# Moving the compressed-attention chain of a sparse-attention layer in between the query projections

## The chip, the cores and the metric

The kernel runs on one core of one Trainium2 chip. The metric is the time of one execution in device microseconds (us); lower is better. The kernel before takes 2796.18 us, the median of three runs (2793.33 to 2796.22).

## The reference

The program is a chain of four blocks, all in float32, on 512 tokens of width 1024: a convolution layer with a feed-forward layer, a sparse-attention layer with a feed-forward layer, and then two mixing layers with memory attention and feed-forward layers. The change is in the sparse-attention layer alone. Cut to what matters there:

```python
# from the stream after the convolution layer
kv = rmsnorm(h, kv_norm) @ w_kv        # k_cmp_raw, v_cmp_raw, k_slc, v_slc, k_win, v_win; 2 groups x 64
def compress(raw, pos, w1, w2):        # 31 overlapping blocks of 32 tokens
    blk = raw[:, :, idx] + pos
    return silu(blk.reshape(B, 2, 31, 32 * 64) @ w1) @ w2
k_cmp, v_cmp = compress(k_cmp_raw, ...), compress(v_cmp_raw, ...)

proj = rmsnorm(x, norm_g) @ w_in       # 16 heads x 64 queries, and 3 x 16 gates
gates = sigmoid(proj[..., 1024:])
# for each of 16 heads
p_cmp = softmax(q @ k_cmp.T * scale - slope * dist) * (a block is visible)
o = g[0] * p_cmp @ v_cmp + g[1] * attention(q, k_slc, v_slc) + g[2] * attention(q, k_win, v_win)
h = h + o @ w_out
```

With 8 blocks of 64 tokens and 16 to be chosen, every block is chosen, so that the selected branch is plain causal attention.

## The kernel before

Every stage is a class with one method per engine (`tensor` for TensorE, `vector`, `scalar`, `gpsimd`, `sync` for the queue that loads weights). `plan` lists the stages; each engine runs through its own methods of all stages in that order, and semaphores tie the engines together. Within an engine nothing is reordered. So the order in which stages and calls are written sets everything around the change.

Dense products run in three passes (`three`, lines 211 to 213): weights and activations are each split into a rounded high part and a low remainder, and high x high, high x low and low x high are added. A panel of weights (128 x 1024) is loaded to `raw`, its high part is made on ScalarE (`split_high`, L188) and its low part on VectorE (`split_low`, L194), four panels ahead of the product that uses it. One product is 24 matmuls of 128x512, and VectorE reads its bank out.

The layer's stages before, in order:

- `KeysValues`: six products of keys and values. Between them, ScalarE and VectorE also split the normed stream for the queries into `xb_high` and `xb_low` (L1334, eight slices).
- `CompressBlocks` (VectorE alone): adds the positions, which gives `cmp_blocks` (L1413, four additions).
- `Project` "w_q": eight query products, evicted by VectorE to `queries` (L1051). Each covers a pair of heads.
- `Gates`: one product of 48 columns (weights `w_gates`), sigmoid on ScalarE, transposition (L1498).
- `StackQueries`: ScalarE rounds all queries at once (L1637), VectorE takes the remainder (L1642).
- `Compress`: the hidden layer of the compression (L1450, 128 small matmuls, which the profile records as 256), silu, the second map (L1459, L1464), and VectorE's copies to `cmp_keys` and `cmp_values` (L1426, L1435).
- `StackKeys`: high and low part of the keys (L1659, L1668).
- `CompressedAttention`: scores for group 0 and 1 (L1551), a softmax for each group on VectorE and ScalarE (L1598 to L1617, exponential L1570), values transposed (L1304) and kept (L1313).
- `BranchAttention`: 32 rounds, two heads times two branches for each of eight pairs. Step s of TensorE is the scores of round s (L1755, L1756), the transposition of the probabilities of round s-2 (`turn`, L1773) and their product with the values of round s-3 (`weigh`, L1795); the first `weigh` of a pair begins with the compressed branch (L1788). VectorE adds the distance bias and takes the maximum (L1862), scales two pieces of the probabilities (L1841) and copies a transposed piece (L1846); ScalarE takes the exponential (L1806) and copies (L1813); GpSimd scales the other two pieces (L1730). The compressed probabilities are transposed in steps 0 and 1 (L1562) and copied by ScalarE (L1574).

## Time and profile before

| | |
|---|---|
| median of the runs | 2796.18 us (2793.33 to 2796.22) |
| the profiled execution | 2795.92 us |
| its span in the trace | 2794.1 us |
| TensorE busy | 2656.0 us, 95% of the span |
| VectorE busy | 1404.7 us, 50% |
| ScalarE busy | 942.2 us, 34% |
| GpSimd busy | 348.7 us, 12% |
| mean granted TensorE clock | 0.965 |

The chain that ended last is 87% TensorE and 8% VectorE. The last query product ends at about 718 us of the span, the gate product at 723.5, and the first transposition of the branch attention begins at 781.1 us; its rounds are regular from 788 to 922 us. A clock of 1.00 in a row is TensorE's full 2.4 GHz, 0.50 is 1.2 GHz.

### The profile page before, as it was taken

How to read it: one execution, taken by the hardware profiler on the slowest of the kernel's cores; microseconds unless marked ns; L12 is line 12 of the kernel's file. 1: busy time of each engine (PE TensorE's matmuls, PEld its weight loads, DVE VectorE, ACT ScalarE, POOL GpSimd, SP SyncE). 2: the span in 40 equal slices, each digit the busy share in tenths (PEclk: the TensorE clock that was granted, in tenths of full speed). 3: DMA queues.
4: the chain of work that ended last, by engine and by line, in shares of the span. 5: the costliest groups of instructions: out<-in, count | busy, mean ns of one | idle time of the engine just before them, and what ended most of it. 6: DMA issues, size and time to landing. Idle time of an engine off the chain costs nothing.

```text
span 2794.1 us, 34029 instructions
## 1 busy us (share of the span) xinstructions
PE 2656.0 (95%) x12132; PEld 2154.5 (77%) x12132; DVE 1404.7 (50%) x2125; ACT 942.2 (34%) x1645; POOL 348.7 (12%) x312
## 2 busy tenths in 40 slices
PE   6988999999889999999989898999999999899999
PEld 5866888877777788888768686788887877688887
DVE  5885544335577544433443565544433656544422
ACT  4554332222366332322233533332222124323221
POOL 2002000110055400012100040200011050200000
PEclk9999999999799999999998998999999998999999
DMA  4201333233200133323321022233322322133322
GB/s 144 75 1 61 100 96 96 75 107 117 65 1 1 46 98 97 93 73 105 100 80 34 16 75 77 69 97 98 92 83 99 99 92 91 46 98 98 94 94 68
DMA packets 61007, 219.83 MB, mean 79 GB/s; under 512 B 7137, under 2 KB 7393, under 8 KB 60401
## 3 DMA queue, kind: packets, MB, share of 16 engines
q1 hardware_dynamic: 58896, 209.15, 24.0%
q0 software_dynamic: 2016, 9.44, 1.0%
q8 instruction: 57, 0.93, 0.1%
q14 instruction: 38, 0.30, 0.0%
HBM read 216.47 MB, written 2.10 MB: 78 GB/s over the span
## 4 chain that ended last, share of the span: by engine, by line
PE 87%; DVE 8%; ACT 2%; issue 2%; POOL 0%; DMA 0%; DVEq 0%; ACTq 0%; SPq 0%; POOLq 0%
PE psum L211 25%; PE psum L213 25%; PE psum L212 25%; DVE conv_out L846 2%; PE psum L1795 2%; PE psum L1773 1%; DVE wl L194 1%; PE psum L1157 1%; PE psum L1209 1%; ACT wh L188 1%; PE psum L1755 1%; PE psum L1756 1%; PE psum L2580 1%; PE psum L1976 1%; DVE xl L747 1%
## 5 line engine op out<-in xcount | busy, mean ns | idle before, releaser
L211 PE MATMUL psum<-xh,wh 128*128 128x512 f32 x1880 | 744.3, 396 | 49.3 <-DVE wl L194 23.0
L212 PE MATMUL psum<-xl,wh 128*128 128x512 f32 x1880 | 739.3, 393 | 0.0
L213 PE MATMUL psum<-xh,wl 128*128 128x512 f32 x1880 | 738.8, 393 | 0.0
L188 ACT ACTIVATE wh<-raw 128x1024 fp32r<-128x1024 f32 x404 | 421.0, 1055 | 793.9 <-PE psum L213 792.0
L194 DVE TENSOR_TENSOR wl<-raw,wh 128x1024 fp32r<-128x1024 f32 x404 | 535.7, 1338 | 261.5 <-ACT wh L188 260.7
L211 PEld LDWEIGHTS psum<-xh,wh 128*128 128x128 f32 x1880 | 357.0, 190 | 129.6 <-DVE xl L747 28.6
L213 PEld LDWEIGHTS psum<-xh,wl 128*128 128x128 f32 x1880 | 356.6, 190 | 76.9 <-issue 0.7
L212 PEld LDWEIGHTS psum<-xl,wh 128*128 128x128 f32 x1880 | 357.0, 190 | 74.6 <-issue 0.6
L211 PE MATMUL psum<-hidden_high,wh 128*128 128x512 f32 x704 | 279.2, 397 | 0.0
L212 PE MATMUL psum<-hidden_low,wh 128*128 128x512 f32 x704 | 279.1, 396 | 0.0
L213 PE MATMUL psum<-hidden_high,wl 128*128 128x512 f32 x704 | 279.0, 396 | 0.0
L692 POOL TENSOR_TENSOR square<-x 128x512 f32 (+1 forms) x72 | 79.3, 1102 | 1240.8 <-DVE x L742 1023.5
L712 ACT ACTIVATE xh<-x,cols (+1 forms) x72 | 52.2, 724 | 457.0 <-DVE x L742 426.2
L742 DVE TENSOR_TENSOR x<-psum,x 128x512 f32 (+1 forms) x72 | 49.5, 688 | 310.8 <-PE psum L213 310.8
L578 DVE TENSOR_TENSOR up<-psum,rstd 128x512 f32<-128x512 f32 x96 | 66.4, 691 | 262.5 <-PE psum L213 262.5
L211 PEld LDWEIGHTS psum<-hidden_high,wh 128*128 128x128 f32 x704 | 132.5, 188 | 34.1 <-DVE wl L194 1.7
L213 PEld LDWEIGHTS psum<-hidden_high,wl 128*128 128x128 f32 x704 | 132.6, 188 | 32.3
L212 PEld LDWEIGHTS psum<-hidden_low,wh 128*128 128x128 f32 x704 | 132.6, 188 | 31.5
L555 ACT ACTIVATE hidden_high<-up 128x512 f32 x88 | 55.6, 632 | 175.8 <-DVE up L589 175.8
L569 DVE TENSOR_TENSOR pre<-psum,rstd 128x512 f32<-128x512 f32 x96 | 66.4, 691 | 75.6 <-PE psum L213 74.4
L1730 POOL TENSOR_SCALAR probs<-probs,small 128x512 f32<-128x512 f32 x64 | 92.0, 1446 | 86.5 <-DVE small L1836 86.4
L593 DVE TENSOR_TENSOR hidden_low<-up,hidden_high 128x512 f32 x88 | 61.0, 693 | 81.8 <-ACT hidden_high L555 81.8
(381 smaller groups left out, 3363.8 us busy)
## 6 DMA issues: line engine op xcount, KB each, us to landing
raw<-ffn_in SPq DMA_DIRECT2D x176, 512.0 KB, 3.5
raw<-ffn_out SPq DMA_DIRECT2D x64, 448.0 KB, 4.1
raw<-ffn_out SPq DMA_DIRECT2D x32, 512.0 KB, 3.5
raw<-pw SPq DMA_DIRECT2D x24, 512.0 KB, 3.6
raw<-o_w_hgg SPq DMA_DIRECT2D x12, 512.0 KB, 4.3
raw<-w_q SPq DMA_DIRECT2D x8, 512.0 KB, 3.8
raw<-w_o SPq DMA_DIRECT2D x8, 512.0 KB, 3.6
raw<-e_w_qk SPq DMA_DIRECT2D x8, 512.0 KB, 3.6
```

The lines of the kernel that those rows point to most:

```text
L188: self.nc.scalar.activation(self.wh[:, slot, :], self.raw[:, slot, :], ACT.Copy).then_inc(self.weights_high.sem, 1)
L194: self.nc.vector.tensor_tensor(self.wl[:, slot, :], self.raw[:, slot, :], self.wh[:, slot, :].bitcast(F32), ALU.subtract).then_inc(self.we ...
L211: nc.tensor.matmul(out, ah, bh, start=start, stop=False)
L212: nc.tensor.matmul(out, ah, bl, start=False, stop=False)
L213: return nc.tensor.matmul(out, al, bh, start=False, stop=stop)
L569: dve.tensor_tensor(c.pre[:, r, :], c.psum[:, bank, :], c.rstd[:], ALU.mult).then_inc(c.banks_freed.sem, 1)
L578: dve.tensor_tensor(c.up[:, r, :], c.psum[:, bank, :], c.rstd[:], ALU.mult).then_inc(c.banks_freed.sem, 1)
L593: dve.tensor_tensor(self.hidden[1][:, at, :], c.up[:, r:r + 1, :], self.hidden[0][:, at, :].bitcast(F32), ALU.subtract).then_inc(self.read ...
L692: pool.tensor_tensor(c.square[:, m % 2, :].rearrange("p (a n) -> p a n", a=1), c.x[:, at, :], c.x[:, at, :], ALU.mult).then_inc(self.squar ...
L846: dve.scalar_tensor_tensor(out, taps, w, out, ALU.mult, ALU.add).then_inc(self.tapped.sem, 1)
L1730: pool.tensor_scalar(p, p, self.stat(3, n)[:, i:i + 1], None, ALU.mult).then_inc(self.scaled_wide.sem, 1)
L1795: mm = pe.matmul(acc[:, t * P:S], self.kv.values[:, b, t, g, window], self.pt[n % self.TURNED][t], start=False, stop=(n % 4 == 3 and t == ...
```

## The change

The compression, the gates, the stacking and the compressed attention stop being stages of their own. `Gates`, `StackedKeys` and `CompressedAttention` become plain helpers, and a new stage `Queries` calls their parts between its eight query products. No matmul is added or removed; the dense products, their panels and their bytes are the same.

- `KeysValues.vector` makes `cmp_blocks` at its last two products. `cmp_pos` is loaded first, under a semaphore of its own.
- TensorE: gate product, hidden layer, query product 0, second map, product 1, transposition of gates and values, product 2, and from then on the compressed scores of one pair of heads behind each product.
- ScalarE and VectorE split the queries pair by pair, and the keys at products 2 and 3. The first softmax runs at products 6 and 7.
- The scores of the last pair, and the whole second softmax, move into `BranchAttention`: VectorE does one piece of it at the end of steps 1, 2, 3, 5, 6 and 7, and the remainder of the last two pairs of queries in steps 4 and 8. Its transpositions come at steps 9 and 10.
- Tiles change places; `probs` and `probs_second` now lie in the arena, the key parts where `ssq`, `square`, `pre` and `up` are.

```diff
 class KeysValues(Stage):          # vector, behind product j
             self.low(dve, j)
+            if j >= 4:
+                self.comp.blocks(dve, j - 4)
...
 class Compress(Stage):
+    def gpsimd(self, pool):
...
+        pool.dma_start(self.pos[:], c.dram["cmp_pos"]).then_inc(self.pos_loaded.sem, 16)
+        for t, n in ((self.w1, "phi_w1"), (self.w2, "phi_w2")):
...
 class CompressedAttention:
+    def load(self, pool, g):
+        if g == 0:
+            pool.wait_ge(self.comp.hidden.sem, 1)
+        else:
+            pool.wait_ge(self.added.sem, g)
+        pool.dma_start(self.bias[:].rearrange("p i (h n) -> p i h n", h=8),
+                       c.dram["cmp_bias"][:, :, 8 * g:8 * g + 8, :]).then_inc(self.loaded.sem, 16)
...
+class Queries(Stage):
...
+    def tensor(self, pe):
+        self.gates.product(pe)
+        self.comp.hidden_layer(pe)
+        for j in range(KD):
+            self.product(pe, j)
+            if j == 0:
+                self.comp.map(pe)
+            if j == 1:
+                self.gates.turn(pe)
+                pe.wait_ge(self.comp.kept.sem, 12)
+                self.kv.turn(pe)
+            if j >= 2:
+                self.cmp.score_pair(pe, j - 2)
+            if j == KD - 1:
+                self.cmp.score_pair(pe, KD - 2)
...
+    def scalar(self, act):
+        self.gates.sigmoid(act)
+        self.comp.silu(act)
+        for j in range(KD):
+            c.ahead(c.split_high, act, self.panel0, j, 0, KD)
+            if j >= 1:
+                self.round(act, j - 1)
+            if j == 2:
+                for k in range(4):
+                    self.keys.round(act, k)
+            if j == 4:
+                self.kv.keep(act, self.keys)
+                act.preload_act_table(ACT.Exp)
+            if j == KD - 1:
+                self.cmp.exp(act, 0)
+        self.round(act, KD - 1)
     def vector(self, dve):
+        self.gates.logits(dve)
+        for j in range(KD):
...            # evict product j to queries
+            c.ahead(c.split_low, dve, self.panel0, j, 0, KD)
+            if j == 0:
+                self.comp.keep(dve)
+            if j == 1:
+                self.gates.keep(dve)
+            if 1 <= j <= KD - 2:
+                self.low(dve, j - 1)
+            if 2 <= j <= 3:
+                self.keys.low(dve, 2 * j - 4)
+                self.keys.low(dve, 2 * j - 3)
+            if j == KD - 2:
+                self.cmp.add(dve, 0)
+                self.cmp.maximum(dve, 0)
+                self.cmp.centre(dve, 0)
+            if j == KD - 1:
+                self.cmp.total(dve, 0)
+                self.cmp.share(dve, 0)
+                self.cmp.scale(dve, 0)
...
 class BranchAttention(Stage):     # tensor
             if s < self.ROUNDS:
                 self.score(pe, s)
-            if s < 2:
-                self.cmp.turn(pe, s)
+            if s == 0:
+                self.cmp.score_pair(pe, KD - 1)
+                for quad in range(2):
+                    self.cmp.turn(pe, quad, 4 + quad)
+            if s in self.LATE_TURNS:          # 9, 10
+                quad = 2 + self.LATE_TURNS.index(s)
...
+                self.cmp.turn(pe, quad, 6)
...                                # scalar
+            if s == 4:
+                self.cmp.exp(act, 1)
...                                # vector, at the end of step s
+    def late(self, dve, s):
+        if s == 1:
+            self.cmp.add(dve, 1)
+        if s == 2:
+            self.cmp.maximum(dve, 1)
+        if s == 3:
+            self.cmp.centre(dve, 1)
+        if s == 5:
+            self.cmp.total(dve, 1)
+        if s == 6:
+            self.cmp.share(dve, 1)
+        if s == 7:
+            self.cmp.scale(dve, 1)
+        if s == 4 or s == 8:
+            self.queries.low(dve, KD - 2 + (s == 8))
...
 plan
-    comp = Compress(c, kv)
-    add(CompressBlocks(comp))
-    qp = add(Project(c, "w_q", KD, kv.parts, kv, norm, q, scale="q_scale"))
-    gates = add(Gates(c, kv, norm))
-    stacked = add(StackQueries(c, q, qp))
-    add(comp)
-    add(keys)
-    cmp_att = add(CompressedAttention(c, q, kv, comp, gates, keys))
+    comp = add(Compress(c, kv))
+    gates = Gates(c, kv, comp)
+    keys = StackedKeys(c, kv, comp)
+    queries = add(Queries(c, kv, comp, gates, keys, norm))
```

What moves on the engines, in the order of the built programs. On TensorE before, behind the gate product (48 columns, L1493's three passes) stand, in one block, the gates' transposition, the hidden layer, the second map, all compressed scores and the values' transposition:

```order
L1498 MATMUL psum<-ident,up 128x48 [waits gates_done]
L1450 MATMUL psum<-cmp_blocks,phi_w_88 64x31 [waits blocked]
L1459 MATMUL psum<-cmp_hidden,phi_w_91 64x31 [waits gates_kept,phi_silu]
L1464 MATMUL psum<-phi_w_91,cmp_hidden 31x64 x8
L1551 MATMUL psum<-cmp_keys,queries 128x64 [waits gates_kept,banks_freed,gates_turned,cmp_kept]
L1304 MATMUL psum<-ident,pre 128x128 [waits banks_freed]
L1755 MATMUL psum<-keys_high,queries_even 128x512 [waits cs_added,k_stacked,q_low]
L1562 MATMUL psum<-ident,cmp_scores 128x128 [waits cs_prob]
```

In the changed kernel the same instructions stand between products (`xb_high,wh` 128x512 is the first matmul of a query product, 48x512 of the gate product; one row for each place):

```order
L212 MATMUL psum<-xb_high,wh 48x512 [waits xb_ready]
L1420 MATMUL psum<-cmp_blocks,phi_w_88 64x31 [waits blocked,phi_loaded]
L212 MATMUL psum<-xb_high,wh 128x512 [waits weights_split,banks_freed]
L1435 MATMUL psum<-cmp_hidden,phi_w_91 64x31 [waits phi_silu]
L1498 MATMUL psum<-ident,up 128x48 [waits cmp_kept,gates_done]
L1305 MATMUL psum<-ident,pre 128x128 [waits banks_freed,cmp_kept]
L1558 MATMUL psum<-cmp_keys,queries 128x64 [waits banks_freed,gates_kept,cmp_kept]
L1863 MATMUL psum<-keys_part_97,queries_even 128x512 [waits q_low,banks_freed,k_stacked]
L1567 MATMUL psum<-ident,cmp_scores_109 128x128 [waits cs_prob]
```

The gate product has moved ahead of the hidden layer and is now the one that waits for `xb_low`; before, the first query product was.

On VectorE at the end of `KeysValues`, before:

```order
L1334 SCALAR_TENSOR_TENSOR xb_low<-x,cols,xb_high 128x512 [waits xb_high_s]
L1356 TENSOR_TENSOR pre<-psum,rstd 128x512 [waits panels_used]
L194 TENSOR_TENSOR wl<-raw,wh 128x1024 [waits weights_high]
L1334 SCALAR_TENSOR_TENSOR xb_low<-x,cols,xb_high 128x512 [waits banks_freed,xb_high_s]
L1413 TENSOR_TENSOR cmp_blocks<-kv_cmp,cmp_pos 128x16x31 [waits banks_freed,phi_loaded]
L1413 TENSOR_TENSOR cmp_blocks<-kv_cmp,cmp_pos 128x16x31 x3
```

and in the changed kernel:

```order
L1335 SCALAR_TENSOR_TENSOR xb_low<-x,cols,xb_high 128x512 [waits xb_high_s]
L1408 TENSOR_TENSOR cmp_blocks<-kv_cmp,cmp_pos 128x16x31 [waits banks_freed,pos_loaded]
L1357 TENSOR_TENSOR pre<-psum,rstd 128x512 [waits panels_used]
L195 TENSOR_TENSOR wl<-raw,wh 128x1024 [waits weights_high]
L1408 TENSOR_TENSOR cmp_blocks<-kv_cmp,cmp_pos 128x16x31 x2
L1335 SCALAR_TENSOR_TENSOR xb_low<-x,cols,xb_high 128x512 [waits banks_freed,xb_high_s]
```

The four additions have moved ahead of the last slices of `xb_low`. On VectorE in step 3 of the branch attention, changed kernel, one piece of the second softmax (`cmp_scores_110`) stands between the copy of a transposed piece and the next round's maximum:

```order
L1957 TENSOR_SCALAR probs_117<-probs_117,small 128x128 [waits at_coef]
L1957 TENSOR_SCALAR probs_second_120<-probs_second_120,small 128x256
L1962 COPY probs_turned_122<-psum 128x512 [waits at_turned]
L1605 TENSOR_TENSOR cmp_scores_110<-cmp_scores_110,cmp_small_112 128x1024
L1995 ISA probs_116,small<-psum,distance 128x512 [waits at_scores,at_turned]
```

Before, nothing stood between the copy (L1846) and the maximum (L1862).

## Rows read from the trace of the kernel before

**Rows 1.** Busy time by stretch (--windows): us, busy us of each engine, clock, DMA

```profile
651.00:712.00 61.00, 61.00 (x266) 49.55 (x266) 36.66 (x43) 15.36 (x18) 0.00 (x0) 1.00 0.32 98
727.00:744.00 17.00, 13.41 (x282) 12.94 (x280) 12.10 (x15) 11.70 (x9) 0.98 (x2) 0.55 0.11 33
744.00:758.00 14.00, 13.97 (x66) 13.97 (x67) 6.19 (x8) 0.53 (x1) 2.85 (x4) 0.50 0.27 94
758.00:788.00 30.00, 18.45 (x78) 16.37 (x77) 21.66 (x59) 16.60 (x47) 6.92 (x5) 0.64 0.00 1
788.00:922.00 134.00, 134.00 (x744) 105.00 (x743) 102.83 (x369) 89.11 (x309) 79.38 (x56) 1.00 0.00 1
```

**Rows 2.** Waits, 723 to 789 us: engine line <- releaser: us, times, longest

```profile
PE psum L1773 <- POOL probs L1730: 6.5, 1, 6.5
PE psum L1551 <- DVE cmp_values L1435: 3.3, 1, 3.3
PE psum L1498 <- ACT up L1506: 3.1, 1, 3.1
PE psum L1562 <- DVE cmp_scores L1617: 3.1, 1, 3.1
```

**Rows 3.** Timeline, TensorE and VectorE, products and their evictions

```profile
712.60 0.75 DVE L1051 SCALAR_TENSOR_TENSOR queries<-psum,cols,rstd 128x512 f32 x1 [3.53 <-PE psum L213]
...
718.23 0.75 DVE L1051 SCALAR_TENSOR_TENSOR queries<-psum,cols,rstd 128x512 f32 x1 [3.53 <-PE psum L213]
...
723.55 0.68 DVE L1512 TENSOR_TENSOR up<-psum,rstd 48x512 f32<-48x512 f32 x1 [3.23 <-PE psum L213]
...
757.74 1.91 PE L1304 MATMUL psum<-ident,pre 128*128 128x128 f32 x8
...
781.11 0.45 PE L1773 MATMUL psum<-ident,probs 128*128 128x128 f32 x1 [6.45 <-POOL probs L1730]
```

**Rows 4.** Timeline of VectorE at the end of the key and value products

```profile
671.61 0.75 DVE L1334 SCALAR_TENSOR_TENSOR xb_low<-x,cols,xb_high 128x512 fp32r<-128x512 f32 x1
...
675.33 2.07 DVE L1334 SCALAR_TENSOR_TENSOR xb_low<-x,cols,xb_high 128x512 fp32r<-128x512 f32 x3
677.31 3.82 DVE L1413 TENSOR_TENSOR cmp_blocks<-kv_cmp,cmp_pos 128x496 f32<-128x496 f32 x4
```

**Rows 5.** Busy time by short stretch in and behind the hidden layer, columns as in Rows 1

```profile
727.50:728.00 0.50, 0.50 (x26) 0.50 (x22) 0.00 (x0) 0.50 (x1) 0.00 (x0) 1.00 0.62 238
...
734.00:736.00 2.00, 2.00 (x44) 2.00 (x41) 1.97 (x2) 1.05 (x1) 0.00 (x0) 0.50 0.00 0
...
768.00:770.00 2.00, 0.84 (x2) 0.65 (x3) 1.97 (x8) 0.00 (x0) 0.00 (x0) 0.50 0.00 0
...
772.00:774.00 2.00, 2.00 (x12) 1.91 (x11) 0.51 (x4) 1.18 (x2) 0.00 (x0) 0.74 0.00 0
```

**Rows 6.** Timeline, VectorE's first softmax and ScalarE's first branch exponential

```profile
761.75 1.21 DVE L1609 TENSOR_REDUCE cmp_small<-cmp_scores 128x32 f32<-128x1024 f32 x1
...
763.88 1.22 DVE L1617 TENSOR_TENSOR cmp_scores<-cmp_scores,cmp_small 128x1024 f32<-128x1024 f32 x1
...
774.03 1.28 ACT L1800 ACT_TABLE_LOAD   x1
775.33 0.72 ACT L1806 ACTIVATE probs<-probs,small 128x512 f32<-128x512 f32 x1
...
778.13 5.81 POOL L1730 TENSOR_SCALAR probs<-probs,small 128x512 f32<-128x512 f32 x4 [28.71 <-DVE small L1836]
```

**Rows 7.** Timeline, regular rounds: VectorE's maximum, GpSimd's scaling

```profile
795.56 0.69 DVE L1862 CUSTOM_DVE_ANT_0 probs<-psum,distance 128x512 f32<-128x512 f32 x1 [0.89 <-PE psum L1756]
800.16 0.69 DVE L1862 CUSTOM_DVE_ANT_0 probs<-psum,distance 128x512 f32<-128x512 f32 x1 [0.96 <-PE psum L1756]
...
797.67 2.88 POOL L1730 TENSOR_SCALAR probs<-probs,small 128x512 f32<-128x512 f32 x2 [1.65 <-DVE small L1836]
```

**Rows 8.** One line each: duration ns min/median/max, first and last start

```profile
L194 DVE TENSOR_TENSOR wl<-raw,wh x404: 1209/1226/2337, 20.5 to 2774.4; 128x1024 fp32r<-128x1024 f32 x135
```

More of the change, by code:

```diff
@@ L1419, in vector, with keep @@
+    def keep(self, dve):
         c = self.c
@@ L1422, in vector @@
         for g in range(2):
-            for h in range(2):
-                q = slice(64 * h, 64 * h + 64)
+            for h, q in enumerate(self.HALVES):
                 scale = c.cols[q, AT["k_scale"] + 4 * g:AT["k_scale"] + 4 * g + 4]
@@ new lines, in gpsimd, with product @@
+    def gpsimd(self, pool):
+        self.cmp.load(pool, 0)
+        pool.dma_start(self.distance[:], self.c.dram["distance"]).then_inc(self.distance_in.sem, 16)
+        self.kv.clear(pool, self.keys)
+        self.cmp.load(pool, 1)
+    def product(self, pe, j):
+        c = self.c
+        ah, al = self.kv.parts
+        n, t = self.panel0 + j, self.product0 + j
+        slot = n % SLOTS
+        after(pe, c.banks_freed, t - (RING_BANKS - 1))
+        pe.wait_ge(c.weights_split.sem, n + 1)
+        for k in range(KD):
+            w = slice(k * P, (k + 1) * P)
+            mm = three(c.nc, c.psum[:, t % RING_BANKS, :], c.wh[:, slot, w], c.wl[:, slot, w], ah[:, k, :], al[:, k, :],
+                       k == 0, k == KD - 1)
+        mm.then_inc(c.panels_used.sem, 1)
@@ new lines, in low @@
+    def low(self, dve, m):
+        for h, own, other in self.halves():
+            dve.wait_ge(self.high.sem, 2 * m + h + 1)
+            dve.tensor_tensor(self.stacked[h][other, m, :], self.q[own, m, :], self.stacked[h][own, m, :].bitcast(F32),
+                              ALU.subtract).then_inc(self.done.sem, 1)
+    def scalar(self, act):
+        c = self.c
+        self.gates.sigmoid(act)
[13 more added lines that the diff above has]
+        self.round(act, KD - 1)
@@ L1748, in score @@
         c, h, b, pair = self.c, n % 2, self.branch(n), n // 4
-        high, low = (k[:, 2 * b + pair // 4, :] for k in self.keys.parts)
+        high, low = (k[2 * b + pair // 4] for k in self.keys.parts)
+        if n % 4 < 2:
+            pe.wait_ge(self.queries.done.sem, 2 * pair + h + 1)
         for i in self.ORDER:
```

361 lines of the change are left out of this document (182 added, 179 removed).

## The prediction

> **What bounds the kernel now.** I read the busy times first: TensorE has no idle time worth the name while the keys, values and queries are projected (61.00 of 61.00 us busy at full clock) and in the regular rounds of the branch attention (134.00 of 134.00) [rows 1]. Between them lie the three stretches from 727 to 788 us, where it is busy 13.41, 13.97 and 18.45 us, at a granted clock of 0.55, 0.50 and 0.64. Two things are to be seen there. First, TensorE waits: 3.1 us for the sigmoid, 3.3 us for the compressed keys and values, 3.1 us for the softmax, 6.5 us for the first scaled probabilities [rows 2]. Second, what it does run is at half clock. The rest of the core is no better used: VectorE and ScalarE pass one small result back and forth. The part that the change can touch runs from the end of the gate product (its eviction starts at 723.55) to the first transposition of the branch attention at 781.11 [rows 3], 57.6 us. Ahead and behind of it TensorE is the limit, and no dense work is added or removed, so the time is won or lost here, and in the attention rounds that take over some of the work.
>
> **The sum.** I count TensorE's time from the start of the first product behind the keys and values. Query products end 5.63 us apart (712.60, 718.23), and the gate product ends at 723.5 [rows 3]; nine of them back to back begin at 723.5 - 50.6 = 672.9. In the changed kernel the end of the eighth query product, which I call T, comes at 723.5 plus what now stands between the products.
>
> 1. *Late remainders, +2.4 us.* VectorE makes `cmp_blocks` (3.82 us) before the last slices of `xb_low` instead of behind them. From 671.61 to 675.33 it has 0.75 + 0.69 + 1.22 us of work, so 1.06 us are idle and take some of the 3.82. The last slice, which ended at 677.4, ends at 677.4 + 3.82 - 1.06 = 680.2 [rows 4]. The gate product wants it for its eighth block, 7 x 0.70 us behind 672.9, at 677.8. TensorE stands for 2.4 us, in two or three pieces. Nothing is queued that could fill them.
>
> 2. *Hidden layer, +8.3 us.* Its 256 recorded passes run at 26 in 0.5 us at full clock and 44 in 2 us at half clock [rows 5], so all of it takes 4.9 or 11.6 us. Before, the clock was full when it began and halved inside it, 3 us of idle TensorE having gone ahead; and it stayed at half through 12 us of these passes and 14 us of the scores, dense as they are [rows 1]. That speaks for small matmuls not holding the clock up. Here no long idle stretch goes ahead, so I expect it to fall some way in, and take the middle.
>
>    A rule that would change this: the Trainium skill, "TensorE: Matmul & The Clock Gate", Part 1, has the clock fall only after an idle stretch and rise with sustained matmuls. By it the hidden layer costs 4.9 us and nothing is to be recovered behind it. The 14 us of busy TensorE at 0.50 stand against it; Part 4 of the same page, by which transpositions do not count as busy in the same way, shows that not every busy time counts.
>
> 3. *Recovery, +2.0 us.* After a restart in 768 to 770 (0.84 us busy) the clock rises within 772 to 774 [rows 5]: some 3.8 us of dense work at half clock, half of it lost. The bounds are 0 (no fall) and 3 us.
>
> 4. *Second map and gates' transposition, +0.8 us:* what is left of 13.41 busy us beside the 11.6 us of the hidden layer, at full clock [rows 1]. *Values' transposition, +0.95 us:* half of 1.91 [rows 3]. *Five pairs of scores ahead of T, +4.4 us:* 64 passes in 13.97 us at 0.50 are 8 pairs of 1.75 us [rows 1], 0.87 at full clock.
>
> T = 723.5 + 2.4 + 8.3 + 2.0 + 0.8 + 0.95 + 4.4 = 742.3. I cost the waits between these at nothing: the map's copies on VectorE, the silu and the sigmoid each have a query product of 5.6 us as cover. VectorE's work for a product is 0.75 (eviction) + 1.23 (weights) [rows 3, 8] + two remainders of a pair, at most 0.75 each [rows 4]: 3.5 us of 6.5; with two key slices 5.0. ScalarE has less. If that cover went, each product would take VectorE's time.
>
> 5. *From T to the first transposition of the branches.* At product 6 VectorE also does three softmax pieces of 1.22 us [rows 6], 7.8 us in all with the links between, against 6.5: product 7 is evicted 1.3 us late and its weights are done at T + 3.3. ScalarE, by then through a panel, a pair of queries and the exponential (some 1.1 to 1.4 us each, from 0.72 for half the elements [rows 6]), lets VectorE go on at T + 3.7. Sum, share and scale took 761.75 to 765.1 before, 3.35 us [rows 6]: T + 7.1. TensorE transposes (0.95), ScalarE copies two tiles (0.6 each, estimated from the same row): T + 9.3. The first exponentials to GpSimd's start took 775.33 to 778.13, 2.8 us, and GpSimd's pair half of 5.81, 2.9 us [rows 6]: T + 15.0 = 757.3. Before it was 781.1. **Gain 23.8 us.** The distances and the bias now come long before they are wanted.
>
> 6. *Attention takes work back, -5 us.* VectorE's idle time ahead of a regular round's maximum is 0.89 or 0.96 us; the maximum starts at 795.56, GpSimd's pair at 797.67, it ends at 800.55, and a round is 4.60 us [rows 7]. Whatever delays the maximum delays GpSimd, and TensorE needs its result in the next step. In steps 3 to 8 the pieces are 1.22 us (0.3 over the slack), in steps 4 and 8 up to 1.5 us (0.6 over): 2 us in all, if the extra product of every fourth round hides a little. Pieces in steps 1 and 2 lie in the filling. Second, the remainders, the centring and the scaling read two tiles in SBUF while GpSimd is at work. L194, of the same kind, takes 1.226 us as a rule and 2.337 at most [rows 8], so such an operation can cost 1.1 us more; there are six. Bounds 0 and 6.7, and I take 3, since GpSimd works 2.88 of 4.6 us.
>
>    The Trainium skill, "SBUF — State Buffer", section "SBUF: two separate sides", says that a VectorE operation with two SBUF inputs and a GpSimd operation that reads SBUF exclude each other for a whole instruction. It leaves open who comes first; if GpSimd were the one to wait each time, the six would cost GpSimd's chain their full length, 7 us by the durations above, near my upper bound.
>
> 7. *Two late transpositions, -0.95 us*, the length of the values' eight [rows 3]. *Clock in the filling, +0.5 us:* before, the clock was below full until 788 [rows 1]; here TensorE idles in shorter pieces. If it stays up, TensorE saves up to 3 us, but VectorE, with its new piece in each step, then sets the pace.
>
> 23.8 - 5 - 0.95 + 0.5 = 18.4 us. The profiled execution took 2795.9, its span 2794.1, 1.8 us around it; 2795.9 - 18.4 = 2777.5. It lies 0.3 under the median of 2796.2, so I say 2778.
>
> **The rivals.**
>
> *The clock stays up.* The hidden layer takes 4.9 and nothing is recovered: 5.4 us less, 2772. For it: no long idle stretch ahead, and the rule above. Against it: 26 us of busy TensorE at half clock [rows 1].
>
> *The late work weighs more.* Every two-input piece costs 1.1 us, and the whole hidden layer runs at half clock (3.3 more): 2778 + 4 + 3 = 2785. For it: GpSimd's chain of 5.0 us is longer than the round of 4.6, so that slack is thin. Against: VectorE idles in each round.
>
> *Slower: VectorE cannot carry the query phase.* If its work for a product exceeded TensorE's 6.5 us, the products would go at its pace. To eat the 18 us it must be 2.3 us longer in each of eight, so 8.8 us; at 10 us a product the kernel would take 2778 + 8 x 3.5 = 2806. I count 3.5 to 5.0 (7.8 once), and GpSimd, the only one it shares ports with, is quiet there. The chance is small.
>
> *The change does nothing.* The chain could be pushed back as a whole, by a wait that I count as covered (the copies to `cmp_values` ahead of the transpositions, say), and TensorE then stands between the products as it stood behind them: 2796. The cover of 5.6 us is longer than any of the four waits [rows 2].
>
> **How the numbers follow.** The forecast has 0.60 (its own range 2773 to 2783), the clock that stays up 0.18, the heavier late work 0.15, slower 0.03, no change 0.02; 0.02 is left to what I don't see, split between faster and slower. The low end is the clock up and no cost of the late work, 2778 - 5.4 - 5 = 2767; the high end is late work at 8.7 and the whole hidden layer and a long recovery at half clock, 2778 + 3.7 + 3.3 + 1 = 2786, and I give 2787. A change of 0.2%, 5.6 us, is about what a measurement of this kernel can tell from none. Faster 0.94, same 0.03, slower 0.03.
>
> **What would show it.** The gate product shows a wait for `xb_low` of 2 to 2.5 us. The hidden layer starts near 681 and takes 5 to 11.6 us; the windows over it tell whether the clock fell, and at which product it came back. Query products are 6.5 us apart without idle time between. T is at 742, the first transposition of the branches at 757. TensorE's wait for GpSimd there, 6.5 us before, is about 3. In steps 3 to 8 the rounds are up to 1 us longer, and L1730's counterpart is what TensorE waits for; if they are regular, point 6 is wrong. The stretch from the first transposition to the end of the rounds is then 4 to 6 us longer than before. The forecast fails if query products are longer than 6.6 us, or T + 15 becomes T + 20 or more.

## The result, and the profile after

The changed kernel took 2770.32 us (median of 4 runs, 2769.73 to 2772.25), the kernel before 2795.56 us beside it (4 runs, 2793.33 to 2796.22): ratio 0.9914, 95% interval 0.9899 to 0.9928. It is faster, by 25 us or 0.9%, where I had forecast 18; the time lies in the range of 2767 to 2787 us and outside the 2773 to 2783 of the likeliest case. The profiled execution took 2769.73 us, its span is 2767.9 us.

Two profiles of one kernel are not alike to the microsecond, so I measure the change by a stretch of its own: from the first load of `ffn_in` ahead of this layer to the first load of `ffn_in` behind it. In SyncE's timeline, of before and of after (start, duration, engine, line):

```profile
231.83 11.54 SPq L182 DMA_DIRECT2D raw<-ffn_in  x3
944.46 0.33 SPq L182 DMA_DIRECT2D raw<-ffn_in  x1
```

```profile
230.09 11.54 SPq L183 DMA_DIRECT2D raw<-ffn_in  x3
918.28 28.38 SPq L183 DMA_DIRECT2D raw<-ffn_in  x6
```

Before it is 712.63 us, after 688.19: the change is worth **24.4 us** here. The 1.74 us by which the first load is earlier come from code that the change does not touch; in the profiles of all kernels below, alike up to there, that load is at 229.5 to 231.8 us. Where I compare times after with times before I add 1.74.

The changed kernel by stretch (columns as in [rows 1]): products of the gates, the hidden layer, queries, filling, first rounds, the other rounds.

```profile
670.90:678.90 8.00, 6.07 (x27) 2.62 (x27) 6.97 (x9) 2.90 (x4) 0.00 (x0) 1.00 0.37 126
678.80:686.40 7.60, 7.60 (x257) 7.54 (x256) 1.91 (x2) 4.25 (x4) 0.00 (x0) 1.00 0.24 73
686.40:738.00 51.60, 51.60 (x272) 42.12 (x269) 30.17 (x45) 19.12 (x27) 4.84 (x7) 1.00 0.29 87
738.00:752.60 14.60, 8.43 (x57) 7.10 (x56) 13.04 (x33) 11.53 (x26) 2.88 (x2) 1.00 0.22 73
752.60:768.00 15.40, 14.98 (x79) 11.92 (x80) 14.49 (x44) 10.22 (x35) 10.01 (x6) 0.89 0.00 0
768.00:896.00 128.00, 126.63 (x705) 99.08 (x704) 102.75 (x361) 86.70 (x300) 76.28 (x52) 1.00 0.00 1
```

The column to look at is the granted clock: 1.00 in every row down to 752.6 us, where [rows 1] had 0.55, 0.50 and 0.64, and 51.60 of 51.60 us busy in the query phase, into which the chain has gone. The three waits of 3 us in [rows 2] are down to one; TensorE's waits of over 0.3 us from 640 to 920 us (engine, line, releaser: us, times, longest) are now

```profile
PE psum L1881 <- POOL probs L1830: 6.0, 6, 3.4
PE psum L1567 <- DVE cmp_scores L1622: 2.6, 1, 2.6
PE psum L212 <- DVE xb_low L1335: 1.9, 2, 1.6
```

The 6.5 us of [rows 2] for the first scaled probabilities are 3.4 (the rest of the 6.0 are five short waits in the rounds). The third row is new: the late remainders. The timeline shows them on VectorE, with the block operands between the last slices of `xb_low`, where [rows 4] had them behind:

```profile
674.02 0.74 DVE L1335 SCALAR_TENSOR_TENSOR xb_low<-x,cols,xb_high 128x512 fp32r<-128x512 f32 x1
674.69 1.90 DVE L1408 TENSOR_TENSOR cmp_blocks<-kv_cmp,cmp_pos 128x496 f32<-128x496 f32 x2
676.50 1.41 DVE L1335 SCALAR_TENSOR_TENSOR xb_low<-x,cols,xb_high 128x512 fp32r<-128x512 f32 x2
```

The hidden layer and the compressed scores in TensorE's timeline, of before and of after (256 matmuls of the hidden layer in each):

```profile
727.03 12.55 PE L1450 MATMUL psum<-cmp_blocks,phi_w 64*64 64x31 f32 x256
...
744.03 13.91 PE L1551 MATMUL psum<-cmp_keys,queries 128*128 128x64 f32 x64 [3.30 <-DVE cmp_values L1435]
```

```profile
678.83 7.65 PE L1420 MATMUL psum<-cmp_blocks,phi_w 64*64 64x31 f32 x256
...
698.92 1.09 PE L1305 MATMUL psum<-ident,pre 128*128 128x128 f32 x8
...
738.00 1.89 PE L1558 MATMUL psum<-cmp_keys,queries 128*128 128x64 f32 x16
...
752.62 0.30 PE L1881 MATMUL psum<-ident,probs 128*128 128x128 f32 x1 [3.42 <-POOL probs L1830]
...
753.72 0.78 PE L1863 MATMUL psum<-keys_part,queries_odd 128*128 128x512 f32 x1
```

The row at 752.62 is the first transposition of the branches, against 781.11 before [rows 3]: with the 1.74 us it is 26.7 us earlier. From there to GpSimd's last scaling (896.04 us; before 922.22) it takes 143.42 us, before 141.11. So 26.7 us are won ahead of the rounds and 2.3 given back in them. Of the 26.7, some 11.7 are the same matmuls at a higher clock: the hidden layer 12.55 and 7.65 us; the 64 passes of the compressed scores 13.91 and 7.89 (the two pairs shown take 1.89, six others 1.00 each); the values' transposition 1.91 [rows 3] and 1.09. The rest is for the most part waiting, which now lies under the products. The last row is the one place where the clock fell in this layer: just behind the 3.42 us of idle time a 512-column matmul lasts 0.78 us, not 0.40.

### The profile page after: what moved, and what is told of

The parts are those of the page before. It is cut to its first block, busy times and chain, and to the rows that moved or that the text cites. A ratio compares the mean times of both kernels' runs of the same rounds, so it can differ in the third digit from the quotient of the medians.

```text
span 2767.9 us, 34006 instructions
## 1 busy us (share of the span) xinstructions
PE 2638.0 (95%) x12132; PEld 2135.8 (77%) x12132; DVE 1406.3 (51%) x2139; ACT 944.3 (34%) x1659; POOL 353.4 (13%) x313
## 4 chain that ended last, share of the span: by engine, by line
PE 86%; DVE 8%; ACT 3%; issue 2%; POOL 0%; DMA 0%; DVEq 0%; ACTq 0%; SPq 0%
PE psum L212 25%; PE psum L213 25%; PE psum L214 25%; DVE conv_out L847 2%; PE psum L1904 2%; DVE wl L195 1%; PE psum L1881 1%; PE psum L1158 1%; PE psum L1210 1%; ACT wh L189 1%; PE psum L2713 1%; PE psum L2109 1%; DVE xl L748 1%; PE psum L1863 1%; PE psum L1864 1%
```

## The experiments

All times below are measured beside runs of the kernel before on the same chip (its medians there were 2794.34 for e1 to e4, 2794.96 for e5 to e8 and 2795.11 us for e9 to e12, and 2795.56 beside the changed kernel, so medians of different groups compare to about 1 us at best). "Stretch" is the one defined above, in the one profile of each kernel.

| kernel | median us (4 runs; e8: 7) | ratio to before | stretch us |
|---|---|---|---|
| before | 2795.56 | 1 | 712.63 |
| after | 2770.32 | 0.9914 [0.9899, 0.9928] | 688.19 |
| after once more (e12) | 2768.82 | 0.9908 [0.9891, 0.9925] | 690.10 |
| e1 idle ahead of the hidden layer | 2781.19 | 0.9951 [0.9935, 0.9968] | 699.17 |
| e2 hidden layer twice | 2777.13 | 0.9937 [0.9921, 0.9954] | 695.61 |
| e3 block operands elsewhere | 2764.04 | 0.9894 [0.9877, 0.9910] | 685.87 |
| e4 filling in another order | 2768.77 | 0.9904 [0.9887, 0.9920] | 688.38 |
| e5 second softmax's pieces left out | 2768.98 | 0.9911 [0.9895, 0.9928] | 686.55 |
| e6 one operand instead of two | 2767.78 | 0.9908 [0.9892, 0.9925] | 687.55 |
| e7 second softmax ahead of the rounds | 2776.61 | 0.9931 [0.9914, 0.9948] | 697.90 |
| e8 before, idle time filled | 2788.38 | 0.9974 [0.9963, 0.9986] | 710.25 |
| e9 as e7, ScalarE's order mended | 2769.82 | 0.9913 [0.9897, 0.9930] | 693.77 |
| e10 filling, another order again | 2769.91 | 0.9911 [0.9895, 0.9928] | 688.07 |
| e11 e3 and e10 together | 2763.59 | 0.9891 [0.9874, 0.9907] | 685.65 |

### e1: idle time ahead of the hidden layer

```diff
         self.gates.product(pe)
+        pe.wait_ge(self.gates.done.sem, 1)
         self.comp.hidden_layer(pe)
```

> The changed kernel with one wait more: TensorE, which has just finished the gate product, waits for the gates themselves before it begins the hidden layer of the compression MLP (the same place as in the kernel before, where the hidden layer started behind an idle TensorE). The gates take about 3 us behind the product. Theory 1, an idle stretch of TensorE just ahead of the small matmuls brings the clock down and dense small matmuls then don't bring it back: the idle time costs about 3 us, the 256 matmuls of the hidden layer go from about 7 us to 10 to 15 us at a granted clock of 0.50 somewhere in them, and the fall may last into the query products: +6 to +15 us against the changed kernel, so that most of its gain in this place is gone. Rival, the small matmuls alone, dense behind wide ones, keep the clock up whatever is ahead of them: only the wait itself, about +3 us, with a granted clock of 1.00 in every stretch from 680 to 740 us.

TensorE's timeline, then three windows of it:

```profile
684.03 13.72 PE L1420 MATMUL psum<-cmp_blocks,phi_w 64*64 64x31 f32 x256 [3.15 <-ACT up L1506]
697.68 0.79 PE L212 MATMUL psum<-xb_high,wh 128*128 128x512 f32 x1
```

```profile
684.00:686.00 2.00, 1.97 (x40) 1.97 (x42) 0.00 (x0) 1.28 (x1) 0.00 (x0) 0.56 0.84 236
690.00:692.00 2.00, 2.00 (x42) 2.00 (x42) 0.00 (x0) 0.00 (x0) 0.00 (x0) 0.50 0.00 0
...
700.00:702.00 2.00, 2.00 (x8) 1.57 (x7) 0.00 (x0) 0.00 (x0) 0.06 (x1) 0.67 0.81 276
702.00:704.00 2.00, 2.00 (x10) 1.64 (x9) 0.00 (x0) 0.00 (x0) 0.00 (x0) 1.00 0.35 125
```

Theory 1 holds. Behind 3.15 us of idle time the clock is at 0.50 almost at once, the hidden layer takes 13.72 us, not 7.65, and in 13.7 us of dense small matmuls it does not come back; it is back by 702, behind the wide ones that begin at 697.68. The wait costs 3.15 us, the matmuls 6.1, the products behind them the rest: 11.0 us in the stretch and 10.9 in the median.

### e2: the hidden layer twice

```diff
-        for j in range(2):
+        for j in (0, 1, 0, 1):
             pe.wait_ge(self.blocked.sem, 2 * j + 2)
```

> The changed kernel with the 256 matmuls of the hidden layer issued twice over, with the same result. Theory 1, small matmuls behind dense ones hold the full clock: the second half costs what the first does, 6.7 us, so +6.5 to +7 us, all at granted clock 1.00. Rival, they held it in the changed kernel only because there were 7 us of them, and a longer row of them lets the clock fall: the second half is dearer, up to 14.6 us for it, and the query products behind it start at half clock: +10 to +18 us.

```profile
680.25 15.12 PE L1420 MATMUL psum<-cmp_blocks,phi_w 64*64 64x31 f32 x512
695.30 0.51 PE L212 MATMUL psum<-xb_high,wh 128*128 128x512 f32 x1
```

15.12 us for 512, 7.47 for the second 256, with the clock at 1.00 in every window: small matmuls that begin at full clock keep it as long as they last here. +7.4 us in the stretch, +6.8 in the median. The 6.7 that I had written were low, for the reason given with step 2 below.

### e3: the block operands made elsewhere

```diff
-            if j >= 4:
-                self.comp.blocks(dve, j - 4)
+            if j == 3:
+                self.comp.blocks(dve, 0)
...
         self.low(dve, 7)
+        self.comp.blocks(dve, 1)
```

> The changed kernel, but the block operands of the gate product are made at other places on VectorE: the first part at the third value product instead of behind the fourth, and the second behind all the low remainders instead of between them. In the changed kernel the three last remainders of the gate product come 1.9, 2 and 1.6 us late for TensorE, because the block operands lie between them. Theory: the 2.3 us that I read as the lateness are given back, since nothing but these remainders holds the product: -1.9 to -2.3 us. Rival: the block operands are needed by the hidden layer at once, and the second part, now behind the last remainder, is as late there (its two instructions take 1.9 us together), so that 0 to -0.5 us is left.

TensorE's waits from 640 to 800 us have no row for `xb_low` left:

```profile
PE psum L1882 <- POOL probs L1831: 3.7, 3, 2.4
PE psum L1568 <- DVE cmp_scores L1623: 2.6, 1, 2.6
```

The stretch is 2.3 us shorter, as expected: the late remainders cost about that (the first transposition comes 2.2 us earlier, counted from the start of the stretch), and the hidden layer does not miss its operands. The median is 6 us lower, more than the theory gives. The surplus is not in this layer: from the `ffn_in` load behind it to the end of the span this profile has 1845.5 us, that of the changed kernel 1849.6. Run e12 comes back to it.

### e4 and e10: another order in the filling

In e4 VectorE takes the first round's maximum ahead of the first softmax's total, share and scale, ScalarE that softmax's exponential ahead of its last panel split, and TensorE turns the first probabilities in round 1; e10 also puts the normalisation of round 0 ahead of round 1's maximum.

```diff
-        dve.wait_ge(self.cmp.probs.sem, 1)
         for s in range(self.ROUNDS + self.OUT_LAG):
-            if s < self.ROUNDS:
+            if s < self.ROUNDS and s != 1:          # e10; e4 has the line as it was
                 self.bias_and_max(dve, s)
+            if s == 0:
+                self.cmp.total(dve, 0)
+                self.cmp.share(dve, 0)
+                self.cmp.scale(dve, 0)
...                                # behind round 0's normalisation
+            if s == 1:
+                self.bias_and_max(dve, 1)           # e10
```

> The changed kernel, with the work between the last query product and the first probabilities of the branch attention put in another order: VectorE does the first round's bias and maximum ahead of the first compressed softmax's total, share and scale; ScalarE does that softmax's exponential ahead of the last panel split; and TensorE turns the first compressed probabilities in round 1 instead of round 0. Theory, the 14.6 us from the last query eviction to the first transposition of the branch attention are a chain in which the compressed softmax's five VectorE pieces lie ahead of the first round's maximum: they leave it, worth about 3 us, of which up to 1 is lost again in round 0 or 1: -2 to -3 us. Rival: GpSimd and ScalarE (its exponentials, a table load, a normalisation of 2.88 us) set the pace from there, so that the first transposition is earlier but the fourth round is not: 0 to -1 us.

> Run e4's order, with the normalisation of round 0 ahead of round 1's maximum on VectorE. In e4 ScalarE's exponentials of round 0 ended at 747.4 us, but VectorE took them up at 749.1, behind the second maximum; GpSimd's first normalisation began at 749.56 us, as in the changed kernel (749.63). Theory, that queue was what held it: GpSimd now begins at 748.0 us and the next layer 1 to 1.5 us earlier. Rival, round 1 then comes later by as much on ScalarE and GpSimd and sets the pace: 0 to -0.5 us.

The rivals come out, not the theories: the stretch is 0.2 us longer in e4 and 0.1 shorter in e10. GpSimd's first three scalings in e10 (its layer starts 0.69 us later than in the profile after):

```profile
748.71 2.89 POOL L1826 TENSOR_SCALAR probs<-probs,small 128x512 f32<-128x512 f32 x2 [10.09 <-DVE small L1952]
754.43 2.88 POOL L1826 TENSOR_SCALAR probs<-probs,small 128x512 f32<-128x512 f32 x2 [2.83 <-DVE small L1952]
759.23 3.77 POOL L1826 TENSOR_SCALAR probs<-probs,small 128x512 f32<-128x512 f32 x2 [1.92 <-DVE small L1952]
```

The first is 1.6 us earlier, as planned, the second and third stand where they stood (753.71 and 758.51 in the profile after). The filling is a chain over all four engines, and its second turn was as tight as its first. Half clock may have a part in it: in e10 the clock is 0.50 from 748 to 752 us, where the changed kernel has 1.00, and in e4 the eight transpositions of the probabilities last 1.97 us, not 1.09. I did not separate the two.

### e5 and e6: what the second softmax costs in the rounds

```diff
-        if s == 2:
-            self.cmp.maximum(dve, 1)
...                                # e5: also centre, total, share, scale
         if s == 7:
-            self.cmp.scale(dve, 1)
+            dve.tensor_reduce(self.cmp.small(2, 1), self.cmp.rows(1), AXX, ALU.max).then_inc(   # e6
+                self.cmp.probs.sem, 1)
```

> The changed kernel with five of the second compressed softmax's six VectorE pieces left out (maximum, subtraction, total, shares, scaling; the sum with its bias stays), so the second half of the compressed attention is computed from unscaled exponentials. It shows what these pieces cost inside the branch attention. Theory 1, which is that of my prediction: VectorE is nearly full there and its 5.5 us of pieces come out as 4.5 us or more, so the kernel is 4 to 5 us faster than the changed kernel. Theory 2, from the trace after: the rounds are paced by TensorE, which waits only 0.2 us at a time, GpSimd's normalisation just slips by 0.9 and 0.5 us in four rounds, and that slip mostly has room: 1 to 2 us faster.

> The changed kernel with the last piece of the second compressed softmax (two operands from SBUF, 128x1024, 1.22 us) put in the same place by a maximum over the same elements, which reads one operand (its result goes into a spare tile; the second half's shares are not multiplied in). VectorE's time there is the same within 0.02 us. Theory, GpSimd is held while VectorE runs a two-operand instruction on SBUF: in this round (the seventh) GpSimd's two normalisations go from 3.77 us back to 2.88 us, while in the third round, where the subtraction still stands, they keep 3.77. Rival, GpSimd is slowed by whatever VectorE does at the time: 3.5 us or more in both. The kernel's time: 0 to 1 us less.

In e5 the rounds (first transposition to GpSimd's last scaling) take 141.84 us, against 143.42: the five pieces cost 1.6 us, so theory 2 holds. e6 tries one of them for its cause. GpSimd's scalings beside the pieces of steps 3 and 7, in the changed kernel the second and in e6 both:

```profile
779.90 3.77 POOL L1830 TENSOR_SCALAR probs<-probs,small 128x512 f32<-128x512 f32 x2 [2.99 <-DVE small L1952]
```

```profile
758.77 3.77 POOL L1830 TENSOR_SCALAR probs<-probs,small 128x512 f32<-128x512 f32 x2 [1.93 <-DVE small L1952]
...
780.18 2.87 POOL L1830 TENSOR_SCALAR probs<-probs,small 128x512 f32<-128x512 f32 x2 [2.98 <-DVE small L1952]
```

In e6 the first, with the two-operand subtraction still beside it, lasts 3.77 us; the second lasted 3.77 in the changed kernel and is back at 2.87 with a one-operand instruction of the same length in its place. The rival falls. Beside these pieces GpSimd is the one that is held: the subtraction itself took 1.21 us. Beside the queries' remainders both are: GpSimd's scaling takes 3.35 us, and the second remainder of each pair 0.96, not 0.69. This agrees with the Trainium skill, "SBUF — State Buffer", section "SBUF: two separate sides": a VectorE instruction with two SBUF inputs and a GpSimd instruction that reads SBUF exclude each other. In this trace it is worth 0.9 us for an instruction of 1.2 us. The rounds of e6 take 142.72 us, 0.7 less.

### e7 and e9: the second softmax ahead of the rounds again

The transpositions of the second softmax go back to step 1 as well (TensorE's part is not shown).

```diff
-        dve.wait_ge(self.cmp.probs.sem, 1)
+        self.cmp.add(dve, 1)
+        self.cmp.maximum(dve, 1)
+        self.cmp.centre(dve, 1)
+        self.cmp.total(dve, 1)
+        self.cmp.share(dve, 1)
+        self.cmp.scale(dve, 1)
         for s in range(self.ROUNDS + self.OUT_LAG):
...                                # scalar; late() keeps the queries' remainders alone
+        self.cmp.exp(act, 1)
         for s in range(self.ROUNDS + self.TURN_LAG):
             if s == 0:
-                self.cmp.copy(act, 0, 4)
-                self.cmp.copy(act, 1, 5)
+                for quad in range(4):               # e9: 2 and 3 behind round 0's exponentials
+                    self.cmp.copy(act, quad, 4 + quad)
```

> The changed kernel with its third part undone: the second compressed softmax (sum, maximum, subtraction, exponential, total, shares, scaling) stands ahead of the branch attention's rounds again, right behind the first. The pieces are 5 instructions of 1.22 us, 0.8 us of small ones and an exponential of 1.06 us, in series: about 8 us on VectorE ahead of the first round's maximum, less what then no longer lies in the rounds. By the prediction's terms (5 us in the rounds) that is +3 us net; by the trace after (about 2 us in the rounds) +5 to +6 us; plus up to 4 us if the longer idle stretch of TensorE brings its clock down for the rounds' small matmuls. A result of 0 or less would say that this part of the change earned nothing.

> The undo of the change's third part (run e7) once more, without a fault of my own in it: there ScalarE copied all four turned blocks ahead of the first round's exponentials and so waited 6.7 us for the two that TensorE turns only in round 1; here it copies the last two behind those exponentials. From the start of the layer to the next layer's first load, run e7 was 9.7 us longer than the changed kernel. Theory: 3.4 us of that were ScalarE's wait, and what is left is the chain itself, 8.1 us of VectorE and ScalarE ahead of round 0, less about 1.8 us in the rounds: 6 to 6.5 us longer than the changed kernel. Rival: the idle stretch of TensorE is as long as before and its clock is low for the first rounds anyway, so that 8 us or more stay.

e7 was 9.7 us longer in the stretch, far over both estimates; ScalarE's timeline showed a fault of the undo, 6.68 us of waiting ahead of round 0's exponentials for blocks turned in round 1. Without it, in e9, the stretch is 5.6 us longer than that of the changed kernel, a little under the 6 to 6.5 expected. TensorE's first transposition of the branches:

```profile
760.13 0.30 PE L1877 MATMUL psum<-ident,probs 128*128 128x128 f32 x1 [1.57 <-issue]
```

With its start aligned that is 7.9 us later than in the changed kernel, and the rounds then take 141.11 us. That this is to the hundredth what they took before is chance: e9 still has the queries' remainders in them, and before had a clock below full until 786 us. The third part of the change earns 7.9 us ahead of the rounds and costs 2.3 in them, 1.6 of it by its pieces (as in e5); the rest lies in the first rounds, where the clock of the changed kernel falls and that of e9 is full. The whole time does not show this: 2769.82 us, as the changed kernel, since from the layer's end on this profile has 1844.0 us against 1849.6. On the layer's own stretch the theory holds; whether anything of the 5.6 us reaches the end of the kernel these four runs leave open.

### e8: the kernel before, with its idle time filled

```diff
         mm.then_inc(c.panels_used.sem, 1)
+        pe.wait_ge(c.banks_freed.sem, self.product0)
+        for i in range(4):
+            pe.matmul(c.psum[:, (self.product0 + 1) % RING_BANKS, :], c.sq["ident"][:], self.q[:, i, :],
+                      start=True, stop=True, skip_group_check=True)
         pe.wait_ge(self.done.sem, 1)
```

> The kernel before, with four dense 128x512 matmuls more, whose result nobody reads, put where TensorE waits for the gates just ahead of the hidden layer (in the kernel before the granted clock fell to 0.50 just behind that idle stretch and stayed there for 256 small matmuls and more). Only the idle stretch is filled; the order of the stages is that of before. Theory, the idle stretch brings the clock down: it now stays at 1.00 and the hidden layer takes 6.7 us instead of 12.5 us; -2 to -5 us against the kernel before, since VectorE's queries and the compressed bias's load still end late. Rival, small matmuls with nothing wide between them bring it down in this place anyway: the clock still falls within the hidden layer, and the time is the same or +1 us. Either way it shows how much of the change's 24 us a full clock alone would have brought.

```profile
722.88 3.59 PE L1498 MATMUL psum<-queries,ident 128*128 128x512 f32 x8
...
726.78 7.65 PE L1450 MATMUL psum<-cmp_blocks,phi_w 64*64 64x31 f32 x256
734.87 0.34 PE L1459 MATMUL psum<-cmp_hidden,phi_w 64*64 64x31 f32 x8 [0.44 <-ACT cmp_hidden L1440]
735.14 0.47 PE L1464 MATMUL psum<-phi_w,cmp_hidden 64*31 64x64 f32 x16
741.88 10.50 PE L1555 MATMUL psum<-cmp_keys,queries 128*128 128x64 f32 x48 [6.27 <-DVE cmp_values L1435]
```

The first row is the filling. The same 256 matmuls, in the same place of the same kernel, take 7.65 us instead of 12.55 once no idle time goes ahead. But of the 4.9 us the wait for `cmp_values` behind them takes 3.0 (6.27 against 3.3 [rows 2]), and in it the clock falls all the same; the stretch is 2.4 us shorter. The median is 6.6 us under that of the kernel before beside it (2794.96), the other 4.2 lying behind the layer (1845.1 us there in this profile, 1849.6 before; see e12). So this filling kept the clock for the hidden layer alone and was worth little: moving the chain under the query products brought the clock and the waits.

### e11 and e12: the best version, and the changed kernel once more

> The orders of e3 (block operands elsewhere) and e10 (normalisation first) together. Theory, they lie on one path, one behind the other, so the gains add: -2.3 us and what e10 shows, 3 to 4 us less than the changed kernel, 2766 to 2767 us. Rival, the 4 us by which e3's profile was shorter still outside this layer were the order's doing and not the clock's in the memory attention: then 2762 us.

> The changed kernel itself, unedited, on the same chip as the two above, to tell their few us from what varies. From the first load of the layer ahead to the first load of the layer behind I expect 688.2 us within 0.3; the whole time 2766 to 2772 us, with what varies lying in the memory attention's granted clock (in the stretch 1670 to 1720 us).

e11 took 2763.59 us (2763.07 to 2764.65), each of its runs below each of e12's (2765.70 to 2770.38). Its stretch is 2.5 us shorter than the changed kernel's: e3's 2.3, and nothing from e10's order, so my sum of the two was wrong; e3 alone is as good. The time itself is lower than the 2766 to 2767 of the theory and nearer the rival's 2762: behind the layer e11 has 1845.4 us and e3 1845.5, 4 us less than the profile after.

e12 is the changed kernel, and its stretch came out 1.9 us longer, outside the 0.3 that I had allowed. GpSimd's third and fourth scalings, in the profile after and in e12:

```profile
758.51 3.77 POOL L1830 TENSOR_SCALAR probs<-probs,small 128x512 f32<-128x512 f32 x2 [1.92 <-DVE small L1952]
763.85 3.35 POOL L1830 TENSOR_SCALAR probs<-probs,small 128x512 f32<-128x512 f32 x2 [1.57 <-DVE small L1952]
```

```profile
759.52 3.77 POOL L1830 TENSOR_SCALAR probs<-probs,small 128x512 f32<-128x512 f32 x2 [1.92 <-DVE small L1952]
766.65 3.35 POOL L1830 TENSOR_SCALAR probs<-probs,small 128x512 f32<-128x512 f32 x2 [3.37 <-DVE small L1952]
```

They are 5.3 us apart in the one and 7.1 in the other. In both the clock falls behind the wait of 3.42 us; it is back by 760 us in the first, later in the second (granted clock from 760 to 764 us: 1.00 and 0.79). So a stretch of this kernel is known to about 2 us, not better. What varies lies in the filling and the first rounds: from GpSimd's fourth scaling to its twelfth, with a clock of 1.00, it takes 41.39 us in the profile after and 41.41 in e12, and 41.37 to 41.39 in e1 to e4, e10 and e11. Over these eight rounds e5 has 39.83 and e6 40.70, so their 1.6 and 0.7 us stand. For e4 and e10 only the rows that they show can be relied on. Behind the layer there is more of it, in the memory attention. TensorE's windows there, of after and of e3:

```profile
1675.00:1685.00 10.00, 9.40 (x54) 9.10 (x55) 3.66 (x8) 0.27 (x1) 0.00 (x0) 0.65 0.01 2
1685.00:1695.00 10.00, 6.83 (x26) 4.44 (x24) 5.89 (x20) 4.25 (x12) 0.00 (x0) 0.69 0.00 1
```

```profile
1675.00:1685.00 10.00, 8.56 (x53) 8.06 (x53) 5.11 (x9) 0.27 (x1) 0.00 (x0) 0.74 0.01 2
1685.00:1695.00 10.00, 7.26 (x25) 4.41 (x26) 6.21 (x26) 5.80 (x18) 0.00 (x0) 0.83 0.01 2
```

The code is the same there (e3 is 1.7 us ahead), but it gets another clock, and from the first load of `xa_wv` to the fifth of `ffn_in` behind it it takes 83.9 us in the one and 81.7 in the other. From the layer's end to the end of the span the 14 profiles have 1844.0 to 1850.1 us, the kernel before 1849.6 and the changed kernel 1849.6 and 1844.5. The time at half clock behind the layer, added up from the clock records, goes with it: 125 us in the six profiles at 1849.5 to 1850.1, 118.5 in the two at 1847.0, 112 to 115 in the six at 1844.0 to 1845.5. Differences of under 6 us between two of these kernels' times can be this alone. Whether an order like e3's makes the shorter kind more frequent stays open: seven of the eight runs of e3 and e11 lie under each of the eight of the changed kernel, but that kernel's own profile e12 is of the shorter kind too.

## Why the prediction was right, and where it was off

The direction and the cause are as forecast: the chain's waits are gone under the query products, and the time is won ahead of the first transposition. The sum was 18.4 us and came out at 24.4, inside the range but outside the likeliest part of it. By its steps, with times after moved by 1.74 us:

- *Late remainders, +2.4:* the gate product takes 7.9 us, not 5.6: 2.3. e3 takes them away and gets 2.3 back. Right.
- *Hidden layer, +8.3:* 7.65. Near by luck, by two errors that cancel. I priced it at 4.9 us full and 11.6 half and took the middle; full is 7.65 and half 13.72 (e1). The counts of [rows 5] take in every instruction that overlaps the window, and one of these lasts longer than the time to the next, so 26 in 0.5 us are not 26 started in it. From start to start it is 29.2 ns (e2: 7.47 us for 256). And the clock did not fall at all.
- *Recovery, +2.0:* 0. This step failed. I had read 26 us at 0.50 in [rows 1] as "small matmuls do not hold the clock up", and here they do: e2 holds it for 15 us, e8 in the very place where before had lost it. What they don't do is bring it back (e1, 13.7 us). The rival "the clock stays up", to which I gave 0.18, was the true one up to T; its 4.9 us for the hidden layer were too low. The rule of the Trainium skill, "TensorE: Matmul & The Clock Gate", Part 1, was right in its first half (the clock falls only after an idle stretch: in this layer the 3.15 us ahead of the hidden layer before, the 3.42 us ahead of the branches after); its second, that sustained matmuls raise it, does not agree with e1, where 13.7 us of the hidden layer's left it at 0.50. Its floor of about 25 ns from start to start in the same part is near the 29.2 measured.
- *Map, transpositions, pairs, +6.15, and the cover of the waits:* 6.6. The products stand 6.5 us apart and TensorE is busy 51.60 of 51.60 us; VectorE carried the phase. My sentence that the cover of 5.6 us is longer than any of the four waits of [rows 2] was wrong for the fourth, 6.5 us; that one is under no product, and 3.4 us of it are left. T was forecast at 742.3 and is 739.7.
- *T to the first transposition, 15.0:* 14.6. Right.
- *Attention takes work back, -5, transpositions -0.95, clock in the filling +0.5:* together 2.3 instead of 5.45. This term was mis-sized. Over the eight rounds from GpSimd's fourth scaling to its twelfth, all at full clock, it takes 38.26 us before, 41.39 after, 39.83 in e5 and 39.79 in e9. So the five pieces cost 1.6, the queries' remainders, which e5 and e9 keep, 1.5, and the two late transpositions, which e5 has there and e9 has not, nothing: 3.1 for the 5.95 of work. The first rounds give 0.8 back, since before had a clock below full until 786 us (I had allowed 0.5 for it). GpSimd's exclusion, its scaling 0.9 us longer in two rounds and 0.47 in two, has a part in the 3.1: e6 shows 0.7 for one of the two of 0.9. How the rest divides between it and VectorE's longer round I did not measure. Two numbers of the working were wrong besides. The 1.1 us for a two-operand instruction came from the longest L194, a time that VectorE lost; in these rounds the subtraction lost none and the most that VectorE lost in a remainder was 0.27. And the full length of the six instructions is some 5.2 us (four of 0.69, two of 1.22), not 7.

2.6 us up to T (0.3 of it because the gate product began that much earlier than I had counted), 0.4 behind T and 3.1 in the rounds make, but for rounding, the 6.0 by which the gain was larger. The time after is another 1.7 us lower because its profile began the layer so much earlier, which is no gain of the change.

Of the rivals, "slower" needed products of 8.8 us and they were 6.5; "the late work weighs more" had a mechanism that is there, the shared access to SBUF, and too high a price.

## What to carry to other kernels

A chain of small dependent steps is best put between dense products of the same engine when the products are longer than any one wait in it: it gains the waits, and also the clock, since idle time just ahead of small matmuls was paid more than once here (e1: 3.15 us of waiting cost 11). Before small work is moved beside another engine's, look which instructions have two operands in SBUF while GpSimd is at work; their cost here lay on GpSimd and hardly in VectorE's busy time. And never divide a window's count by its length when instructions last longer than their spacing: take the first start and the last end.

## What the runs showed of the hardware that I had not expected

The granted clock has a memory that is not symmetric for small matmuls: 64x31 ones, dense, hold 1.00 for 15.12 us, and held at 0.50 they stay there for 13.7 us, until 512-column ones begin. Between two profiles of the changed kernel the time from the fall to the rise of the clock in the filling differs (from 760 to 764 us it is 1.00 in one and 0.79 in the other), and with it this layer by 1.9 us. Behind the layer the two have 1849.6 and 1844.5 us, with 125 and 115 us at half clock.
